# A 64-byte pad behind a decoder kernel's weight rings in SBUF

## What is computed

```python
h = rmsnorm(x, norm1_g) * (1 + sc1) + sh1       # sc, sh, gt: six products of silu(c) with w_ada
z = h @ w_in                                    # 1024 x 3340, split among three head groups
x = x + gt1 * (concat(hgrn2(z), rg_lru(z), gated_deltanet(z)) @ w_out)
h = rmsnorm(x, norm2_g) * (1 + sc2) + sh2
x = x + gt2 * peer(h)
```

## Time and profile before

| | |
|---|---|
| median of 3 runs | 2345.74 us (2343.91 to 2347.03) |
| the profiled execution | 2351.11 us, of which its span is 2349.2 us |
| TensorE, matmuls | 2255.1 us busy, 96% of the span, 20,514 matmuls |
| VectorE / ScalarE / GpSimd | 64% / 54% / 45% |
| mean granted TensorE clock | 0.975 of full speed |

### The profile page before, as it was taken

How to read it: one execution, slowest core, us unless ns; L and a number is a source line. 1 busy time by engine, 2 the same in 40 slices (tenths; PEclk the granted TensorE clock), 3 DMA queues, 4 the chain that set the end, 5 groups by cost and what they waited for, 6 DMA issues and landing times. The chain is left out here.

```text
span 2349.2 us, 57915 instructions
## 1 busy us (share of the span) xinstructions
PE 2255.1 (96%) x20514; PEld 2082.3 (89%) x20514; DVE 1496.3 (64%) x3099; ACT 1269.2 (54%) x2439; POOL 1055.4 (45%) x960
## 2 busy tenths in 40 slices
PE   6979999999999999999999799999999999999998
PEld 4946779999998799999979377799999978999997
DVE  3756527963225968888666663499422287887885
ACT  3534215567557855555556332355765587555554
POOL 0021007874446646566300210288544475665661
PEclk9988899999999999999999789999999999999999
DMA  7472035556555189899644702355555533998992
GB/s 285 155 251 91 12 137 169 180 179 205 187 187 171 58 270 311 284 302 312 207 163 157 265 30 83 126 180 180 197 188 187 188 125 127 302 314 275 312 306 101
DMA packets 123814, 455.52 MB, mean 194 GB/s; under 512 B 13744, under 2 KB 14256, under 8 KB 122544
## 3 DMA queue, kind: packets, MB, share of 16 engines
q1 hardware_dynamic: 105264, 386.80, 46.5%
q0 software_dynamic: 18432, 67.12, 10.5%
HBM read 449.37 MB, written 4.49 MB: 193 GB/s over the span
## 5 line engine op out<-in xcount | busy, mean ns | idle before, releaser
L430 POOL TENSOR_TENSOR parts<-ring,parts 128x512 fp32r<-128x512 f32 x358 | 465.6, 1303 | 468.9 <-ACT parts L423 455.4
L423 ACT ACTIVATE parts<-ring 128x512 fp32r<-128x512 f32 x620 | 388.9, 631 | 349.8 <-PE ps_u L477 280.8
L473 PE MATMUL ps_u<-h_parts,parts 128*128 128x256 f32 x4096 | 563.5, 280 | 1.0 <-ACT parts L423 0.6
L2692 PE MATMUL ps_y<-act_parts,parts 128*128 128x256 f32 x4096 | 563.0, 279 | 0.0
L473 PEld LDWEIGHTS ps_u<-h_parts,parts 128*128 128x128 f32 x4096 | 514.1, 188 | 3.5 <-ACT parts L423 2.2
L2692 PEld LDWEIGHTS ps_y<-act_parts,parts 128*128 128x128 f32 x4096 | 514.9, 188 | 0.8 <-ACT parts L2632 0.7
L430 DVE TENSOR_TENSOR parts<-ring,parts 128x512 fp32r<-128x512 f32 x262 | 181.8, 697 | 371.1 <-ACT parts L423 346.2
L2741 POOL TENSOR_TENSOR act_parts<-big,act_parts 128x256 fp32r<-128x256 f32 x256 | 246.4, 963 | 303.5 <-ACT act_parts L2721 303.5
L477 PE MATMUL ps_u<-h_parts,parts 128*128 128x256 f32 x2048 | 323.2, 279 | 1.0 <-DVE parts L430 0.7
L2696 PE MATMUL ps_y<-act_parts,parts 128*128 128x256 f32 x2048 | 323.0, 279 | 0.0
L477 PEld LDWEIGHTS ps_u<-h_parts,parts 128*128 128x128 f32 x2048 | 274.8, 188 | 2.0 <-DVE parts L430 1.1
(11 more groups left out here) (409 smaller groups left out, 2816.4 us busy)
## 6 DMA issues: line engine op xcount, KB each, us to landing
ring<-in_stream SPq DMA_DIRECT2D x506, 512.0 KB, 3.4
more_ring<-in_stream SPq DMA_DIRECT2D x126, 512.0 KB, 5.1
extra_ring<-in_stream SPq DMA_DIRECT2D x32, 512.0 KB, 5.4
mod_ring<-in_stream SPq DMA_DIRECT2D x32, 512.0 KB, 3.2
big<-in_stream SPq DMA_DIRECT2D x16, 512.0 KB, 11.7
out_state_out<-big SPq DMA_DIRECT2D x2, 1440.0 KB, 6.9
big<-in_state SPq DMA_DIRECT2D x2, 1280.0 KB, 10.6
big<-in_mixc SPq DMA_DIRECT2D x2, 1024.0 KB, 8.1
```

What stands on the lines that cost most here:

```text
L423: eng.activation(m.parts[:, q % PARTS, 0, :], half_tile(m, t, half), ACT.Copy).then_inc(s["hi_ready"], 1)
L430: eng.tensor_tensor(m.parts[:, q % PARTS, 1, :], half_tile(m, t, half), m.parts[:, q % PARTS, 0, :].bitcast(F32), ALU.subtract).then_inc(m ...
L473: pe.matmul(out, hi[:, k, :], hr[:, side, kk, 0:tokens], start=(kk + side == 0), stop=False)
L2692: pe.matmul(ps[:, half * KD // 2 + k, :], hi[:, k, :], act_parts[:, j % AHEAD, side, :], start=False, stop=False)
```

## The change

One tensor is allocated between `small` and `mod`. Nothing reads or writes it.

```diff
@@ -242,6 +242,7 @@
         self.mod_ring = nc.alloc_sbuf_tensor_at("mod_ring", [P, PARTS, D], F32, offset=parts_at)
         self.keep = sb("keep", [P, KEEP_W])
         self.small = sb("small", [P, SMALL_W])
+        self.line_end = sb("line_end", [P, 16])
         self.mod = sb("mod", [P, 6 * KD, 1 + NB])
         self.gain = sb("gain", [P, 2, KD, 1 + NB])
         self.cond = sb("cond", [P, KD, COND])
```

## The result

The changed kernel took 2383.61 us in the median of 3 runs (2381.29 to 2390.90) against 2345.74: a ratio of 1.0151, 95% interval 1.0120 to 1.0183. It is 38 us slower. The profiled execution took 2390.9 us around a span of 2388.8 us, 39.8 us more than the one before. The forecast was 2319 us, faster; the time lies outside the range, on the other side.

A forecast was written before the change was run, and what follows sets the result against it. The prediction took the kernel to be bound by TensorE's matmul count times their step. From 2351.1 us it took 26.5 us for faster split products, giving 2324.6, and set 2319 us because the runs' median lies 5.4 lower; range 2284 to 2374.

The forecast's parts named there:

- What bounds the kernel: In the long stages, time is the number of TensorE matmuls times the distance from one start to the next.
- The terms set to nothing: Vector, scalar and GpSimd operands, DMA landings and plain float32 products: each counted as 0.
- The split float32r products: 12,288 matmuls of 256 and 1,296 of 288 columns in experts, combining and projection: 26.5 us gained, at best 106.
- I take a quarter of the excess: 1.9 ns of 7.6: Each 256-column split product gets 1.9 ns faster, of 7.6 ns above the 109.3 its columns would cost.
- there is more room below than the trace shows above: Reason for expecting a gain: the excess is in all three families of split products and never below 7 ns.
- three half tiles named as signs: Twelve matmuls after the change: 1.38 us if right, 1.40 if distance is nothing, 1.42 if one more meeting.
- The nearest rows: One-hot products at distance 0 with equally dense weight loads: an excess of only about 1 ns.
- all of them change alike: All 13,584 split matmuls have one and the same distance modulo 128, which goes from 32 to 96.
- The rival on the other side: Moving stream meets the weights once more per split matmul: 1.9 ns each, 26 us slower, 2372 us; chance 26%.
- The rule weighed in the prediction: TensorE's two read ports are independent and weight loads take no read bandwidth, so the pad changes nothing.

The follow-up runs named there:

- e1: Kernel before with the 64-byte pad behind `big`, so only the tensors a stage allocates for itself moved: 2389.3 against 2353.4 us, ratio 1.0163.
- e7: Kernel before plus a block of TensorE alone in the stages' order and strides, distances 32 to 272 bytes; 288, 352, 368 repeated the steps of 32, 96, 112.
- e9: Block of TensorE alone with 32 or 64 float32r weight columns, then plain float32: 113.3 to 120.0 ns for 256 columns with 32 weight columns.
- e6: Pad of 128 bytes instead of 64 in the change's place, against the kernel before: 2362.2 against 2351.9 us, ratio 1.0043.
- e8: Kernel before with `x_parts`, `h_parts` and `act_parts` shifted 80 bytes inside their allocations, distance 112: 2310.7 against 2349.3 us, ratio 0.9830.
- e11: Changed kernel with the three operands beginning 16 bytes later inside their allocations, distance 112: 2313.6 against 2350.1 us for the kernel before, ratio 0.9853.
- e5: Kernel before plus a block of TensorE alone, distances in 4-byte steps, other column counts and strides: distance 112 gave 113.3 ns, 116 gave 122.5 and 122.8.

## Why the prediction was wrong

- **What bounds the kernel: right.** The time is the number of split products times their step. 12,288 x (120.0 - 116.9) ns is 38 us and 1,296 x 0.5 ns is 0.6 us, against 39.6 us of span; 116.9 is the mean of the steps in the four long stages of before, by the starts in its trace; their two steady values are 116.7 and 117.8 ns (which read 116.7 and 117.5). About 2 of these 38 us come off again, because TensorE's pauses between tiles got shorter, which leaves the 36.1 us above.
- **The terms set to nothing: right.** ScalarE's splits didn't change, VectorE's went from 844 to 834 ns (twice the 5 ns that were allowed for) on an engine that waits, the plain float32 products stayed. e1 shows that the loss needs no move of `big` or the small tensors.
- **The step that failed is "The split float32r products"**, "I take a quarter of the excess: 1.9 ns of 7.6", with a minus sign. It measured plus 3.1 ns. The prediction called the sign a choice and gave as its reason that "there is more room below than the trace shows above". That room was mis-sized. Of the 7.6 ns, 4.2 are the floor of 113.3 ns against the 109.2 of bf16 (e7 and e9), and none of the distances tried won them. What could be won was about 3.5 ns, and what could be lost 5 to 6, since the sweeps go up to 122.8. Among the 16 distances of e7 only one is below the 116.7 ns of before, and 14 are above (64 and 192 reached 113.3 in other groups). A sample of one distance, already low, was read as if it were high. None of the three half tiles named as signs, 1.38, 1.40 and 1.42 us, came: it was 1.44.
- **The nearest rows said nothing of distance.** The small excess of the one-hot products at distance 0 was taken as a sign that another distance can be nearly free. e9 has plain float32 of 128 columns at 111.7 ns at all six distances, and the one-hot products, by their starts in the trace of before, run at 111 to 112 ns: that step does not go by the distance at all.
- **The period was wrong.** The prediction counted modulo 128. e6 and e7 show 256. The projection's steps of 1152 bytes are 128 modulo 256, so "all of them change alike" was untrue there: their distances alternate between two values, and their step moved by only 0.5 ns.
- **The rival on the other side had the place and the direction**, with 26%; its price of 26 us was too small (38), and its account, one more meeting of the two streams, was not borne out: with a quarter of the weights, or with weights that stay in one place, distances still differ by up to 6.7 ns. That it is the distance of the two operands is shown. How 113.3 comes of one distance and 120.0 of another stays open. So does what the floor belongs to: of the moving operand, float32r takes 1024 bytes a partition in 113.3 ns, bf16 512 in 109.2 and plain float32 1024 in 215.8, so these runs do not tell the number format from the pace of reading. That every second element takes twice the time, and one repeated element less than the floor, speaks for the reading.
- **The rule weighed in the prediction** (Trainium skill, SBUF — State Buffer, section "Who interferes with whom": TensorE never waits for anyone; and TensorE: Matmul & The Clock Gate, section "What happens when you issue a matmul": loading the next weights takes nothing from the running matmul) holds here for bf16 and plain float32, 109.2 and 215.8 ns at all distances tried. For float32r it doesn't: 113.3 to 122.8 ns by the distance between weights and moving operand, with TensorE alone.

## What to carry to other kernels

Where float32r matmuls run back to back and each loads new weights, read the step from one start to the next off the timeline and compare it with 17/16 of what the columns take at full clock (seen for 256 and 512 columns; 288 never came under 131.1 ns, where that would be 127.5); what is above that may hang on the distance between moving and stationary operand. One block of TensorE alone, swept in steps of 16 bytes over 256, finds a good place in a single run. It can miss one, as e7 did at 64 and 192, so the choice has to be timed in the kernel. The place is worth pinning, since any tensor allocated between the two moves it. A pad tensor can't set the distance 112 here, because each start is rounded up to 32 bytes: e8 and e11 begin the operands later inside their allocations. A trace shows one distance only, so it bounds neither the gain nor the loss of another.

## What the runs showed that was not expected

- Moving operands 80 bytes further (distance 112) gained 1.7%, and 64 bytes further lost 1.5%, on the same kernel.
- The steps are locked patterns. The kernel before has two, 116.7 and 117.8 ns, and the kernel at distance 64 has 117.8 and 113.3 ns within one stage (1.41 and 1.36 us a half tile). Executions can differ by what they fall into: in layer 1's combining stage nearly half of the half tiles of the kernel before and of e5 are at 117.8 ns, and none of e7, whose layers are the same code at the same distance. There it is 1.6 us. In e6, whose steps range from 117 to 119 ns in its profiled execution, that execution took 25 us more than the profiled one of before, and the median of its runs 10 us more; that patterns are the reason was not shown.
- Float32r with a moving operand of adjacent elements had a floor of 17 cycles for 16 columns at 2.4 GHz: 113.3 ns for 256 columns and 226.7 for 512, where bf16 takes 109.2 and 215.9.
- A float32r moving operand of every second element took twice the time of adjacent ones, 226.7 to 228.9 ns for 256 columns (e5).
- With 128 new float32r weights each, matmuls of 128 and of 192 columns had the same step, 111.7 ns; plain float32 had it too, with 128.
